# The hi and lo parts of each weight slab placed value by value side by side, in a two-block fp32 transformer kernel on one core

## Chip, core and metric

One core of one Trainium2 chip. The metric is the device time of one launch in microseconds. A DMA engine group feeds SBUF, TensorE multiplies out of SBUF into PSUM, and VectorE, ScalarE and GpSimd do the elementwise work.

## What is computed

The reference runs two blocks over 256 tokens (272 with 16 meta tokens) of width 1024, all in float32:

```
n1 = rmsnorm(h); xr, gr, cq, ckv, kr, g_rnn, g_att = split(n1 @ w_in)
y_rnn = (rg_lru(causal_conv(xr)) * gelu(gr)) @ w_rnn_out
y_att = attention(cq, ckv, kr) @ w_attn_out
h += (sigmoid(g_rnn) * y_rnn + sigmoid(g_att) * y_att) @ w_out
h += peer(rmsnorm(h))          # 16384 experts, 8 heads x 16 chosen per token
x = rmsnorm(h)[:, 16:]
for layer in (0, 1):           # a convolution layer, then an attention layer
    x += 0.5 * rmsnorm(swiglu(rmsnorm(x)))
    x += rmsnorm(mixer(rmsnorm(x)))
    x += 0.5 * rmsnorm(swiglu(rmsnorm(x)))
```

PEER is done densely: scores of all experts, `gelu(n2 @ u.T)`, are multiplied by a sparse coefficient and then by `v`.

## The kernel before

**Weights as a stream.** All weight matrices are cut into 128x128 tiles and laid in HBM in the order in which TensorE uses them (`Plan`), eight tiles to a slab of 512 KB. `Ring` runs the slabs on each engine's own instruction stream: SP loads slab `s` into one of three `raw` buffers (`fetch`), ScalarE rounds it to fp32r (`split_hi`, L392, one instruction of 1024 values to a partition; it waits until TensorE is done with the slab four before), and VectorE, or for every third slab of a long stretch GpSimd, subtracts to get what the rounding left (`split_lo`, L409). TensorE takes tiles with `Weights.take` (L341 to L348).

**Three products to a tile.** Each value is a hi and a lo part, and `mm3` (L323) makes hi*hi, hi*lo and lo*hi: the tile's hi part is loaded twice and its lo part once. Every product is one weight load of 128x128 and one matmul of 256 columns (272 in the first stage). So the tile of weights is the stationary operand and the activations (`n1`, `n2`, `xg`, `bn`, `akv`, `hh`, `o`, `ql`: pairs of hi and lo in fp32r) are moving. In three stretches it is the other way round: the first block's values (`ukv_v`, read as 4 tiles side by side), PEER's `v` (1024 columns, in matmuls of 512) and the last block's values (`wv`). There activations stand in the array, and the slab moves. In PEER's `v` stretch what stands is the coefficients `c`, of which three buffers turn over (`split_coef` on ScalarE and VectorE).

**Where things lie.** `whi0..3` and `wlo0..3` are eight areas of 4096 bytes a partition, one behind the other; a tile is 512 bytes in each, read with a step of 4 bytes. The areas placed after them start as follows, counted from `whi0` and modulo 256 bytes: `hh`, `akv`, `n2` and `c` at 0, `bn` and `xg` (placed from the top of SBUF) at 64; `n1` has rows of 1088 bytes and so takes on 0, 64, 128 and 192.

**Order of the work.** Each engine's order is written out by hand; `ring.to(...)` puts the slab work between the others at fixed places. TensorE's order is: first block (with 192 tiles of `gr`, `g_rnn`, `g_att` as filler between the attention heads), `w_out`, PEER's queries, `u` (128 columns of 8 tiles, with one-hot bf16 products of 64 columns in bursts of 24 that build coefficients), `v` (again with such bursts in its first half), then the second block: feed-forward 0, convolution, feed-forward 1 and 2, attention, feed-forward 3.

Of the kernel before, what the change touches and what calls it, by code (L numbers as in the profile page):

```python
# [14 lines left out]
ACT = mybir.ActivationFunctionType  # L15
ALU = mybir.AluOpType
AX = mybir.AxisListType
BF16 = mybir.dt.bfloat16
F32 = mybir.dt.float32
F32R = mybir.dt.float32r  # L20
# [3 lines left out]
NC = D // 128  # L24
NMETA = 16
NX = 256
# [5 lines left out]
PH, PK, NKEY = 8, 16, 128  # L32
NU = 2 * PH
CW, DWW = 4, 31
SLAB = 8
NRAW, NSPLIT = 3, 4
# [27 lines left out]
TG, NCF = 8, 3  # L64
# [16 lines left out]
class Plan:  # L81
# [23 lines left out]
    def col(self, key, name, c, n=NC):  # L105
        self.run(key, [(name, k, c) for k in range(n)])
# [89 lines left out]
PLAN = Plan()  # L196
NSLAB = PLAN.nslab
# [11 lines left out]
    return (10 <= s <= 18 and s % 2 == 0) or (21 <= s <= 345 and s % 3 == 0) or (417 <= s <= 431 and s % 3 == 0)  # L209

LO_AT = {}
_n = {"lo_v": 1, "lo_p": 0}
# [64 lines left out]
class Kernel:  # L279
# [25 lines left out]
    def place(self, name, shape, dt=F32, top=False):  # L305
# [8 lines left out]
        assert self.low <= self.high, name  # L314
        return self.nc.alloc_sbuf_tensor_at(name, shape, dt, offset=at)

    def col(self, name, c):
        return self.par[:, PCOL[name] + c:PCOL[name] + c + 1]

# [15 lines left out]
class Weights:  # L335
# [5 lines left out]
    def take(self, name, row, c, n=1):  # L341
        k, (s, j) = self.k, divmod(self.pos, SLAB)
        assert j + n <= SLAB and PLAN.order[self.pos:self.pos + n] == [(name, row, c + i) for i in range(n)]
        q, v = LO_AT[s]
        k.P.wait_ge(k.s[q], 1 if self.pos + n <= SLAB // 2 else v)
        self.pos += n
        cols = slice(j * 128, (j + n) * 128)
        return k.whi[s % NSPLIT][:, cols], k.wlo[s % NSPLIT][:, cols]  # L348

    def end(self, ins, pos=None):  # L350
        if (self.pos if pos is None else pos) in PLAN.ends:
# [21 lines left out]
class Ring:  # L373
# [6 lines left out]
    def split_hi(self):  # L380
        k, s, A = self.k, self.his, self.k.A
        self.his += 1
        if self.me is not A:
            return
        A.e.wait_ge(k.raw_in[s % NRAW], 16 * (s // NRAW + 1))
        if s == 0:
            for c in (slice(0, SLAB * 64), slice(SLAB * 64, SLAB * 128)):
                k.s["hi"].inc(k.act(k.whi[0][:, c], k.raw[0][:, c], ACT.Copy))
            return
        if s >= NSPLIT:  # L390
            A.wait_ge(k.s["tiles"], PLAN.count[SLAB * (s - NSPLIT + 1)])
        k.s["hi"].inc(k.act(k.whi[s % NSPLIT][:, :], k.raw[s % NRAW][:, :], ACT.Copy))  # L392

    def split_lo(self):
        k, s, me = self.k, self.los, self.me
        self.los += 1
        if me is k.S:
            return self.fetch(s + NRAW)
        q = LO_AT[s][0]
        if me is not (k.G if q == "lo_p" else k.V):  # L400
            return
        raw, hi, lo = k.raw[s % NRAW], k.whi[s % NSPLIT], k.wlo[s % NSPLIT]
        if s == 0:
            for i, c in enumerate((slice(0, SLAB * 64), slice(SLAB * 64, SLAB * 128))):
                me.wait_ge(k.s["hi"], i + 1)
                k.s[q].inc(me.e.tensor_tensor(lo[:, c], raw[:, c], hi[:, c].bitcast(F32), ALU.subtract))
            return
        me.wait_ge(k.s["hi"], s + 2)
        k.s[q].inc(me.e.tensor_tensor(lo[:, :], raw[:, :], hi[:, :].bitcast(F32), ALU.subtract))  # L409

    def fetch(self, s):
        k = self.k
# [39 lines left out]
def tensors(k):  # L452
    k.H = k.place("H", [128, NC, T])
    k.par = k.place("par", [128, PCOL["wdw"]])
    k.ident = k.place("con", [128, 128])[:, :]
    k.ones = k.place("ones", [128, 128])[:, :]
    k.std = k.place("std", [128, 8])[:, :]
    k.rcol = k.place("rcol", [128, 8])[:, :]
    k.junk = k.place("junk", [128, 1])[:, :]
    k.acc = k.place("acc", [128, NX])[:, :]  # L460
    k.eps6 = k.place("eps6", [128, 1])[:, :]
    k.eps5 = k.place("eps5", [128, 1])[:, :]
    k.half = k.place("half", [128, 6 * NC])
    k.raw = [k.place(f"raw{i}", [128, SLAB * 128]) for i in range(NRAW)]
    k.whi = [k.place(f"whi{i}", [128, SLAB * 128], F32R) for i in range(NSPLIT)]
    k.wlo = [k.place(f"wlo{i}", [128, SLAB * 128], F32R) for i in range(NSPLIT)]
    k.X = [k.H[:, c, NMETA:T] for c in range(NC)]
    low, high = k.low, k.high
    block1_tensors(k)
    k.low, k.high = low, high  # L470
    peer_tensors(k)
    k.low, k.high = low, high
    block2_tensors(k)
# [885 lines left out]
def peer_tensors(k):  # L1359
    p = k.p = Box()  # L1360

    p.iT = [k.place(f"iT{a}", [128, NX, 2], BF16)[:, :, :] for a in range(2)]
    p.gp = k.place("gp", [128, NG, 3, TG, 2], BF16)
    p.io = k.place("iota16", [128, NKEY // 2, 2], BF16)[:, :, :]
    p.c = [k.place("c0", [128, 2, NX], F32R)]
    low = k.low
    p.n2 = k.place("n2", [128, NC, 2, NX], F32R)
    p.kh, p.kl = k.place("kh", [128, 2, NKEY], F32R), k.place("kl", [128, 2, NKEY], F32R)
    p.q2 = k.place("q2", [128, 2, 2, NX], F32R)

    k.low = low
    ohA1 = [k.place(f"ohA{i}", [128, TG, NKEY], BF16)[:, :, :] for i in range(2)]
    ohB1 = [k.place(f"ohB{i}", [128, 3 * TG, HK], BF16)[:, :, :] for i in range(2)]
    oh1 = k.place("oh1", [128, TG, HK], BF16)[:, :, :]
    p.c += [k.place(f"c{i}", [128, 2, NX], F32R) for i in range(1, NCF)]

    act2 = k.place("act2", [128, HK * NX], F32, True)
    high = k.high
    p.xg = k.place("xg", [128, NC, 2, NX], F32R, True)
    p.sqs = k.place("sqs", [128, NC, NX], F32, True)  # L1380
    p.rb = k.place("rb", [128, NX], F32, True)[:, :]

    k.high = high
    act1 = k.place("act1", [128, HK * NX], F32, True)
    p.halves = [act1, act2]
    p.chunks = [(act1, act2)[e // HK][:, e % HK * NX:(e % HK + 1) * NX] for e in range(NKEY)]


    at_ = [0]

    def scr(n, dt=F32):
        a = act2[:, at_[0]:at_[0] + n]
        at_[0] += n
        return a.bitcast(dt) if dt is not F32 else a

    p.sc = scr(2 * NU * NKEY).rearrange("p (a u n) -> p a u n", a=2, u=NU)
    p.t12 = scr(2 * NU * PK).rearrange("p (a u n) -> p a u n", a=2, u=NU)
    p.i12 = scr(2 * NU * PK, U32).rearrange("p (a u n) -> p a u n", a=2, u=NU)
    p.f12 = scr(2 * NU * PK).rearrange("p (a u n) -> p a u n", a=2, u=NU)
    p.cand = [scr(256) for _ in range(2)]  # L1400
    p.cand2 = [scr(256) for _ in range(2)]
    p.rep = [scr(128) for _ in range(2)]
    p.top = scr(NU * PK).rearrange("p (u n) -> p u n", u=NU)
    p.sel = scr(NU * PK, U32).rearrange("p (u n) -> p u n", u=NU)
    p.sab = [scr(NU * PK, U32).rearrange("p (u n) -> p u n", u=NU) for _ in range(2)]
    p.fab = [scr(NU * PK).rearrange("p (u n) -> p u n", u=NU) for _ in range(2)]
    p.hot = scr(4 * PK * PK).rearrange("p (u j a) -> p u j a", u=4, j=PK)
    p.iab = [scr(NU * PK).rearrange("p (u n) -> p u n", u=NU) for _ in range(2)]
    p.gs = scr(NU * PK).rearrange("p (u n) -> p u n", u=NU)
    p.gsum = scr(NU)  # L1410
    p.io128 = scr(NKEY)
    p.kraw = scr(2 * NKEY).rearrange("p (a n) -> p a n", a=2)
    assert at_[0] <= (TAIL - HK) * NX

    bf = act2[:, (TAIL - HK) * NX:].bitcast(BF16)
    part = lambda o, n: bf[:, o * TG:(o + n) * TG].rearrange("p (t i) -> p t i", t=TG)
    ohA0 = [part(i * NKEY, NKEY) for i in range(2)]
    ohB0 = [bf[:, (2 * NKEY + 3 * i * HK) * TG:(2 * NKEY + 3 * (i + 1) * HK) * TG].rearrange("p (t i) -> p t i", i=HK)
            for i in range(2)]
    p.ohA, p.ohB, p.oh1 = [ohA0, ohA1], [ohB0, ohB1], [part(2 * NKEY + 6 * HK, HK), oh1]  # L1420
    p.xg_pair = [(p.xg[:, c, 0, :], p.xg[:, c, 1, :]) for c in range(NC)]
    p.n2_pair = [(p.n2[:, c, 0, :], p.n2[:, c, 1, :]) for c in range(NC)]
    p.c_pair = [(c[:, 0, :], c[:, 1, :]) for c in p.c]


    k.low = low
    p.y = k.place("y", [128, 2, D])
    p.yT = [k.PS[:, 4 + m // 2, NX * (m % 2):NX * (m % 2) + NX] for m in range(NC)]
# [662 lines left out]
def block2_tensors(k):  # L2091
# [12 lines left out]
    c = z.conv = Box()  # L2104
# [2 lines left out]

    def ffn_tensors(i):
        f = Box()
        f.hh = k.place(f"hh{i}", [128, NFF, 2, NX], F32R)  # L2110
        f.gsc, f.sil, f.hf = (k.place(f"{n}{i}", [128, 3, NX]) for n in ("gsc", "sil", "hf"))
        f.x = [(f.hh[:, j, 0, :], f.hh[:, j, 1, :]) for j in range(NFF)]
        return f
# [9 lines left out]
    k.low, k.high = low, high  # L2123
    z.ffn.append(ffn_tensors(1))
    k.low = low
    z.akv = k.place("akv", [128, NC, 2, NX], F32R)
    z.kvn = [(z.akv[:, c_, 0, :], z.akv[:, c_, 1, :]) for c_ in range(NC)]
    low2 = k.low
    z.ffn.append(ffn_tensors(2))
    k.low = low2  # L2130
    a = z.att = Box()
# [1115 lines left out]
```

## Time and profile before

| | |
|---|---|
| median of 3 runs | 2185.61 us (2181.64 to 2186.68) |
| the profiled execution | 2189.28 us |
| its span, first to last instruction | 2187.9 us |
| TensorE, share of the span with a matmul in it | 97%, 17080 matmul records |
| VectorE, ScalarE, GpSimd | 74%, 55%, 26% |
| DMA | 352.86 MB read, 49% of 16 engines |
| mean granted clock of TensorE | 0.990 |

A matmul record lasts from its issue to its last result, so records overlap and a "busy" TensorE says nothing of its pace. The pace is read from the times between starts. Time between the span and the whole execution is 1.4 us.

### The profile page before, as it was taken

To read this page: it belongs to the slowest core of one execution; us is meant where nothing else is said; L and a number is where in the kernel's file an instruction comes from. 1 tells how busy PE (TensorE), PEld (TensorE's weight loads), DVE (VectorE), ACT (ScalarE), POOL (GpSimd) and SP (SyncE) were. 2 spreads that over 40 slices of the span, in tenths; PEclk is the share of its full clock that TensorE was granted. 3 is DMA by queue.
4 is the path that set the end of the run, shared out by engine and by line. 5 is a ranking of instruction groups with operands and counts; after the bars stand their busy time and mean duration, and the time that the engine had idled before them with its cause. 6 is when DMAs were issued, how large, how long until landed. Compare 5 with 4: busy or idle time off the path is not lost.

```text
span 2187.9 us, 41590 instructions
## 1 busy us (share of the span) xinstructions
PE 2129.9 (97%) x17080; PEld 2033.4 (93%) x17080; DVE 1612.8 (74%) x2603; ACT 1195.2 (55%) x2106; POOL 570.7 (26%) x386
## 2 busy tenths in 40 slices
PE   9999999999999999999999999989999999999997
PEld 9898999999999988888889998979999999899997
DVE  7887767798988399975567647968656764788664
ACT  6776656454433444445567755865445544566453
POOL 7432245233222233333333002242001101113001
PEclk9999999999999999999999999999999999999999
DMA  5433455555444554555545554224554555534553
GB/s 172 151 126 106 146 169 168 185 177 188 158 156 151 177 162 159 172 183 192 194 165 184 186 193 133 77 81 153 191 193 144 193 184 193 181 129 159 190 192 114
DMA packets 101131, 357.15 MB, mean 163 GB/s; under 512 B 12048, under 2 KB 15440, under 8 KB 100816
## 3 DMA queue, kind: packets, MB, share of 16 engines
q1 hardware_dynamic: 100080, 352.35, 49.0%
q8 instruction: 136, 2.23, 0.4%
q10 hardware_dynamic: 864, 2.16, 0.3%
q14 instruction: 51, 0.42, 0.1%
HBM read 352.86 MB, written 1.05 MB: 162 GB/s over the span
## 4 chain that ended last, share of the span: by engine, by line
PE 82%; DVE 10%; ACT 3%; issue 2%; DMA 2%; POOL 1%; SPq 0%; POOLq 0%; ACTq 0%; DVEq 0%
PE PS L321 81%; DVE wlo L409 2%; DMA raw<-stream 2%; DVE w L2782 1%; DVE H L2715 1%; ACT whi L329 1%; DVE bn L2666 1%; DVE H L2713 1%; DVE ohA L1877 1%; POOL wlo L409 1%; DVE gate L1223 0%; ACT bsq L329 0%; ACT L329 0%; DVE gate L1234 0%; POOL XC L1304 0%
## 5 line engine op out<-in xcount | busy, mean ns | idle before, releaser
L409 DVE TENSOR_TENSOR wlo<-raw,whi 128x1024 fp32r<-128x1024 f32 x546 | 688.2, 1263 | 225.3 <-ACT whi L329 224.4
L329 ACT ACTIVATE whi<-raw 128x1024 fp32r<-128x1024 f32 (+1 forms) x667 | 698.7, 1050 | 170.0 <-PE PS L321 99.7
L321 PE MATMUL PS<-bn,whi 128*128 128x256 f32 x3328 | 597.1, 281 | 14.7 <-DVE bn L2666 5.0
L321 PEld LDWEIGHTS PS<-bn,whi 128*128 128x128 f32 x3328 | 510.9, 188 | 20.6 <-issue 10.2
L321 PE MATMUL PS<-n,whi 128*128 128x256 f32 (+1 forms) x2784 | 519.1, 288 | 8.0 <-DVE wlo L409 3.7
L409 POOL TENSOR_TENSOR wlo<-raw,whi 128x1024 fp32r<-128x1024 f32 x119 | 325.4, 2734 | 684.8 <-ACT whi L329 684.8
L321 PE MATMUL PS<-bn,wlo 128*128 128x256 f32 x1664 | 460.0, 280 | 0.0
L321 PEld LDWEIGHTS PS<-n,whi 128*128 128x128 f32 x2784 | 438.2, 193 | 12.1 <-DVE wlo L409 3.9
L321 PE MATMUL PS<-n,wlo 128*128 128x256 f32 (+1 forms) x1392 | 396.8, 285 | 0.0
L321 PE MATMUL PS<-whi,c 128*128 128x512 f32 x1024 | 324.2, 393 | 0.6 <-ACT act L329 0.6
L321 PEld LDWEIGHTS PS<-bn,wlo 128*128 128x128 f32 x1664 | 313.4, 188 | 0.0
L321 PEld LDWEIGHTS PS<-n,wlo 128*128 128x128 f32 x1392 | 269.1, 193 | 0.0
L321 PE MATMUL PS<-hh,whi 128*128 128x256 f32 x1408 | 253.6, 283 | 0.0
L321 PEld LDWEIGHTS PS<-whi,c 128*128 128x128 f32 x1024 | 192.3, 188 | 40.0 <-issue 0.7
L321 PEld LDWEIGHTS PS<-hh,whi 128*128 128x128 f32 x1408 | 219.6, 192 | 0.0
L321 PE MATMUL PS<-hh,wlo 128*128 128x256 f32 x704 | 199.2, 283 | 0.0
L321 PE MATMUL PS<-wlo,c 128*128 128x512 f32 x512 | 199.2, 389 | 0.0
L329 ACT ACTIVATE act<-PS 128x256 f32<-128x256 f32 x128 | 49.3, 385 | 210.8 <-PE PS L321 210.7
L329 ACT ACTIVATE c<-act 128x256 fp32r<-128x256 f32 x128 | 53.4, 418 | 188.5 <-PE PS L321 188.4
L332 DVE TENSOR_TENSOR c<-act,c 128x256 fp32r<-128x256 f32 x128 | 87.3, 686 | 91.1 <-ACT c L329 90.5
L321 PEld LDWEIGHTS PS<-hh,wlo 128*128 128x128 f32 x704 | 135.1, 192 | 0.0
L1986 POOL TENSOR_TENSOR acc<-bsq 128x256 f32<-128x256 f32 x12 | 10.2, 850 | 470.2 <-ACT bsq L329 470.2
(355 smaller groups left out, 2918.6 us busy)
## 6 DMA issues: line engine op xcount, KB each, us to landing
raw<-stream SPq DMA_DIRECT2D x666, 512.0 KB, 3.3
abias<-c_alibi ACTq DMA_DIRECT2D x1, 1536.0 KB, 6.9
H<-xt SPq DMA_DIRECT2D x4, 256.0 KB, 6.0
out<-H SPq DMA_DIRECT2D x3, 256.0 KB, 2.2
mask<-c_mask SPq DMA_DIRECT2D x1, 272.0 KB, 6.2
K<-Vh SPq DMA_DIRECT2D x2, 136.0 KB, 4.0
K<-Vl SPq DMA_DIRECT2D x2, 136.0 KB, 4.7
out<-H ACTq DMA_DIRECT2D x2, 128.0 KB, 1.9
```

Of the source, the lines that this page charges most:

```text
L321: return self.nc.tensor.matmul(out, l, r, start=start, stop=stop, skip_group_check=True)
L329: return self.nc.scalar.activation(out, in_, func, **kw)
L332: return self.nc.vector.tensor_tensor(out, x, hi.bitcast(F32), ALU.subtract)
L409: k.s[q].inc(me.e.tensor_tensor(lo[:, :], raw[:, :], hi[:, :].bitcast(F32), ALU.subtract))
L1877: step(vec.tensor_tensor(pairs(p.ohA[half][g % 2]), keys(p.iT[1], NKEY), iota(0, NKEY), ALU.is_equal))
L1986: s["acc"].inc(pool.tensor_tensor(k.acc, sq[:, 0, :] if c == 1 else k.acc, sq[:, c, :], ALU.add))
L2666: s["pre_lo"].inc(k.nc.vector.scalar_tensor_tensor(x[:, c, 1, :], k.X[c], pre_gain(k, pre, c), x[:, c, 0, :].bitcast(F32), ALU.mult, ALU.s ...
L2713: V.step(vec.tensor_tensor(k.X[c], k.X[c], z.rp, ALU.mult))
L2715: s["x_new"].inc(vec.tensor_tensor(k.X[c], k.X[c], z.F[:, c, :], ALU.add))
L2782: ins = vec.scalar_tensor_tensor(c.w[:, q, :], c.u[:, q, t:t + NX], z.wdw[:, j:j + 1], c.w[:, q, :], ALU.mult, ALU.add)
```

## The change

Nothing is added, removed or moved in any engine's instruction stream; operands' addresses and steps change.

1. A slab's two parts share one area of 8192 bytes. For slabs whose tiles stand in the array ("paired"), value `i` of hi is at `8i` and that of lo at `8i + 4`: ScalarE writes and VectorE or GpSimd reads and writes with a step of 8 bytes, and TensorE loads a tile with that step. For slabs up to the end of the first block's values, for PEER's `v` and for `wv` the two parts lie apart as before (`halves`).
2. PEER's coefficients `c0..c2` are laid in pairs too, so the weight loads of the `v` stretch have a step of 8 bytes, while the slab moves with a step of 4.
3. `phase(128)` moves `c`, `n2`, `hh` and `akv` so that they start 128 bytes further, modulo 256, from the start of the slab areas. `bn` and `xg` stay at 64, `n1`, `o` and `ql` stay where they were.

```diff
+def paired(s):
+    streams = [(0, (PLAN.at["v", 1] + 7) // SLAB), (PLAN.at["v_", 0] // SLAB, (PLAN.at["v_", NKEY - 1] + 7) // SLAB),
+               (PLAN.at["wv"] // SLAB, (PLAN.at["wv"] + NC * NC - 1) // SLAB)]
+    return not any(a <= s <= b for a, b in streams)
...
+    def phase(self, n):
+        self.low += (n - self.low + self.weights) % 256
...
-        return k.whi[s % NSPLIT][:, cols], k.wlo[s % NSPLIT][:, cols]
+        return k.split[s][:, cols, 0], k.split[s][:, cols, 1]
...
-        k.s["hi"].inc(k.act(k.whi[s % NSPLIT][:, :], k.raw[s % NRAW][:, :], ACT.Copy))
+        k.s["hi"].inc(k.act(k.split[s][:, :, 0], k.raw[s % NRAW][:, :], ACT.Copy))
...
-        raw, hi, lo = k.raw[s % NRAW], k.whi[s % NSPLIT], k.wlo[s % NSPLIT]
+        raw, hi, lo = k.raw[s % NRAW], k.split[s][:, :, 0], k.split[s][:, :, 1]
...
-        k.s[q].inc(me.e.tensor_tensor(lo[:, :], raw[:, :], hi[:, :].bitcast(F32), ALU.subtract))
+        k.s[q].inc(me.e.tensor_tensor(lo, raw[:, :], hi.bitcast(F32), ALU.subtract))
...
-    k.whi = [k.place(f"whi{i}", [128, SLAB * 128], F32R) for i in range(NSPLIT)]
-    k.wlo = [k.place(f"wlo{i}", [128, SLAB * 128], F32R) for i in range(NSPLIT)]
+    w = [k.place(f"w{i}", [128, 2 * SLAB * 128], F32R) for i in range(NSPLIT)]
+    pairs = [x[:, :].rearrange("p (n q) -> p n q", q=2) for x in w]
+    halves = [x[:, :].rearrange("p (q n) -> p n q", q=2) for x in w]
+    k.split = [(pairs if paired(s) else halves)[s % NSPLIT] for s in range(NSLAB)]
...
-    p.c = [k.place("c0", [128, 2, NX], F32R)]
+    by_part = lambda x: x[:, :, :].rearrange("p t q -> p q t")
+    k.phase(128)
+    p.c = [by_part(k.place("c0", [128, NX, 2], F32R))]
     low = k.low
+    k.phase(128)
     p.n2 = k.place("n2", [128, NC, 2, NX], F32R)
...
-    p.c += [k.place(f"c{i}", [128, 2, NX], F32R) for i in range(1, NCF)]
+    k.phase(128)
+    p.c += [by_part(k.place(f"c{i}", [128, NX, 2], F32R)) for i in range(1, NCF)]
...
+        k.phase(128)
         f.hh = k.place(f"hh{i}", [128, NFF, 2, NX], F32R)
...
+    k.phase(128)
     z.akv = k.place("akv", [128, NC, 2, NX], F32R)
```

## Rows read from the trace of the kernel before

**Rows 1.** The page, busy us of each engine, share of the span, count.
```profile
PE 2129.9 (97%) x17080; PEld 2033.4 (93%) x17080; DVE 1612.8 (74%) x2603; ACT 1195.2 (55%) x2106; POOL 570.7 (26%) x386
```
**Rows 2.** Waits of TensorE, the largest: us in total, times, longest.
```profile
PE PS L321 <- DVE wlo L409: 6.4, 3, 3.7
```
**Rows 3.** Timeline of TensorE from 600.01 us, PEER's `u`, `n2` moving: start us, us, xcount.
```profile
600.01 0.40 PE L321 MATMUL PS<-n,whi 128*128 128x256 f32 x2
...
601.45 0.87 PE L321 MATMUL PS<-act 128*128 128x64 bf16 x24
```
**Rows 4.** The same from 1725.73 us, feed-forward, `bn` moving.
```profile
1725.73 0.28 PE L321 MATMUL PS<-bn,wlo 128*128 128x256 f32 x1
...
1727.14 0.28 PE L321 MATMUL PS<-bn,wlo 128*128 128x256 f32 x1
```
**Rows 5.** The same from 1801.81 us, feed-forward, `hh` moving.
```profile
1801.81 0.40 PE L321 MATMUL PS<-hh,whi 128*128 128x256 f32 x2
...
1802.89 0.40 PE L321 MATMUL PS<-hh,whi 128*128 128x256 f32 x2
```
**Rows 6.** The same from 1000.04 us, PEER's `v`, `c` standing.
```profile
1000.04 0.39 PE L321 MATMUL PS<-wlo,c 128*128 128x512 f32 x1
...
1001.40 0.39 PE L321 MATMUL PS<-wlo,c 128*128 128x512 f32 x1
```
**Rows 7.** The same from 270.07 us, first block, `n1` moving.
```profile
270.07 0.28 PE L321 MATMUL PS<-n,wlo 128*128 128x256 f32 x1
...
271.84 0.28 PE L321 MATMUL PS<-n,wlo 128*128 128x256 f32 x1
```
**Rows 8.** Groups of instructions by form: xcount | busy us, mean ns | idle before.
```profile
L321 PE MATMUL PS<-act 128*128 128x64 bf16 x768 | 27.9, 193 | 0.0
L321 PE MATMUL PS<-bn,whi 128*128 128x256 f32 x3328 | 597.1, 281 | 14.7 <-DVE bn L2666 5.0 <-ACT bn L329 4.5 <-DVE wlo L409 2.7
L321 PE MATMUL PS<-hh,whi 128*128 128x256 f32 x1408 | 253.6, 283 | 0.0
L321 PE MATMUL PS<-whi,c 128*128 128x512 f32 x1024 | 324.2, 393 | 0.6 <-ACT act L329 0.6
L321 PE MATMUL PS<-xg,whi 128*128 128x256 f32 x256 | 48.0, 282 | 0.0
L321 PE MATMUL PS<-akv,whi 128*128 128x256 f32 x256 | 47.7, 285 | 2.0 <-DVE akv L2666 1.2 <-ACT akv L329 0.8
L321 PE MATMUL PS<-o,whi 128*128 128x256 f32 x256 | 45.8, 282 | 0.6 <-DVE o L332 0.6
```
**Rows 9.** Timeline and groups: transposes of 128 columns in float32, first block.
```profile
101.05 0.60 PE L716 MATMUL PS<-con,Sm 128*128 128x128 f32 x4
L716 PE MATMUL PS<-con,Sm x64: 270/272/421, 101.1 to 225.0; 128*128 128x128 f32 x64
```
**Rows 10.** Groups of instructions: the slab's splitting, and two of 512 values on VectorE.
```profile
L329 ACT ACTIVATE whi<-raw 128x1024 fp32r<-128x1024 f32 x665 | 697.5, 1051 | 168.6 <-PE PS L321 99.7 <-DMA raw<-stream 62.9 <-DVE gp L1865 2.1
L409 DVE TENSOR_TENSOR wlo<-raw,whi 128x1024 fp32r<-128x1024 f32 x546 | 688.2, 1263 | 225.3 <-ACT whi L329 224.4
L409 POOL TENSOR_TENSOR wlo<-raw,whi 128x1024 fp32r<-128x1024 f32 x119 | 325.4, 2734 | 684.8 <-ACT whi L329 684.8
L332 DVE TENSOR_TENSOR PT<-PS,PT 128x512 fp32r<-128x512 f32 x16 | 10.8, 676 | 0.8 <-ACT PT L329 0.4
L1890 DVE TENSOR_TENSOR act<-PS,act 128x512 f32<-128x512 f32 x64 | 43.6, 682 | 0.0
```
**Rows 11.** Stretches of time: us, busy us (count) of PE, PEld, DVE, ACT, POOL, clock, DMA share, GB/s.
```profile
450.00:500.00 50.00, 50.00 (x419) 50.00 (x419) 49.69 (x99) 26.48 (x38) 15.51 (x7) 1.00 0.55 179
550.00:600.00 50.00, 50.00 (x593) 49.57 (x593) 49.13 (x55) 20.00 (x30) 13.36 (x5) 1.00 0.47 159
600.00:650.00 50.00, 50.00 (x594) 49.53 (x593) 43.30 (x50) 18.94 (x30) 12.54 (x5) 1.00 0.48 159
650.00:700.00 50.00, 50.00 (x612) 49.57 (x611) 47.93 (x54) 19.78 (x30) 13.24 (x5) 1.00 0.45 149
1500.00:1600.00 100.00, 100.00 (x851) 100.00 (x851) 73.53 (x111) 50.77 (x75) 10.24 (x8) 1.00 0.58 189
```
**Rows 12.** DMA issues: xcount, KB each, median us from issue to landing.
```profile
raw<-stream SPq DMA_DIRECT2D x666, 512.0 KB, 3.3
```

More of the change, by code:

```diff
@@ L387, in split_hi @@
             for c in (slice(0, SLAB * 64), slice(SLAB * 64, SLAB * 128)):
-                k.s["hi"].inc(k.act(k.whi[0][:, c], k.raw[0][:, c], ACT.Copy))
+                k.s["hi"].inc(k.act(k.split[0][:, c, 0], k.raw[0][:, c], ACT.Copy))
             return
@@ L463, in tensors @@
     k.half = k.place("half", [128, 6 * NC])
+    k.weights = k.low
     k.raw = [k.place(f"raw{i}", [128, SLAB * 128]) for i in range(NRAW)]
-    k.whi = [k.place(f"whi{i}", [128, SLAB * 128], F32R) for i in range(NSPLIT)]
-    k.wlo = [k.place(f"wlo{i}", [128, SLAB * 128], F32R) for i in range(NSPLIT)]
+    w = [k.place(f"w{i}", [128, 2 * SLAB * 128], F32R) for i in range(NSPLIT)]
+    pairs = [x[:, :].rearrange("p (n q) -> p n q", q=2) for x in w]
+    halves = [x[:, :].rearrange("p (q n) -> p n q", q=2) for x in w]
+    k.split = [(pairs if paired(s) else halves)[s % NSPLIT] for s in range(NSLAB)]
     k.X = [k.H[:, c, NMETA:T] for c in range(NC)]
```

## The prediction

> **What bounds the kernel now.** I read the engines' shares first: TensorE has a matmul in flight for 97% of the span, VectorE works for 74%, ScalarE for 55% [rows 1]. Then TensorE's waits: the largest releaser costs it 6.4 us in total [rows 2]. So almost nothing outside TensorE sets the time, and the question is TensorE's own pace. Busy time can't give it, since records overlap; the starts can. Each product is one weight load and one matmul, and start to start it takes:
> - `n2` moving: 12 matmuls in 601.45 - 600.01 = 1.44 us, 120.0 ns each [rows 3]
> - `hh` moving: 9 in 1.08 us, 120.0 ns [rows 5]
> - `bn` moving: 12 in 1.41 us, 117.5 ns [rows 4]
> - `n1` moving, first block: 15 in 1.77 us, 118.0 ns [rows 7]
> - `c` standing, 512 columns moving: 6 in 1.36 us, 226.7 ns [rows 6]
>
> From 256 to 512 columns the pace grows by 106.7 ns, 0.417 ns a column, which is the 2.4 GHz level at a granted clock of 1.00 [rows 11]. What is left above the columns' own time is 120.0 - 106.7 = 13.3 ns at 256 and 226.7 - 213.4 = 13.3 ns at 512. The bf16 burst of 64 columns shows how small that can be: 24 matmuls in 0.87 us, of which the last lasts 0.193 [rows 3, 8], so (0.87 - 0.193) / 23 = 29.4 ns each, and 29.4 - 26.7 = 2.7 ns above the columns. So the fp32r products pay 13.3 - 2.7 = 10.6 ns more than the burst does, and with `bn` 10.8 - 2.7 = 8.1 ns.
>
> Two things speak about what these 8 to 11 ns are. They do not shrink when the matmul gets twice as long, so a weight load too long to hide behind the matmul is not it. And they depend on where the moving operand lies: `n2` and `hh`, at 0 modulo 256 from the slabs, give 120.0; `bn`, at 64, gives 117.5. A cost that follows the addresses of two operands points to their two reads meeting in SBUF. The moving read goes at 4 bytes in 0.417 ns. If the weight read takes its 128 values in about the time of the 256 columns, it goes at 4 bytes in 0.83 ns, half as fast in bytes, so the faster one overtakes it again and again, wherever the two begin. With a step of 8 bytes the weight read advances through memory as fast as the moving one, and the distance between them stays what it was at the start. That is what the change would do, and `phase(128)` sets the distance.
>
> **The sum.** No instruction is added or moved, so everything lies in durations.
>
> TensorE. Matmuls that get a stepped weight load, with the lo groups half as many as the hi groups [rows 8]: `bn` 3328 + 1664 and `xg` 256 + 128, together 5376; `hh` 2112; `akv` 384; `c` 1536; `n2` 128 x 8 x 3 = 3072; and in the first block 384 with `o`, 256 tiles x 3 = 768 with `n1`, 126 with `ql` and 42 with `kvl`, together 1320. In all 13,800. If the whole excess goes:
> - 5376 x 8.1 ns = 43.5 us
> - (3072 + 2112 + 384) x 10.6 = 59.0 us
> - 1536 x 10.6 = 16.3 us
> - 1320 x (118.0 - 109.4 = 8.6) = 11.4 us
>
> together 130 us. Bounds: nothing from below if the excess is something else, and a loss if the stepped load is slower (rivals). I take nearly the whole, since the nearest row with no excess, the burst, shows that the array itself does not need it.
>
> What takes some of it back:
> - VectorE. In PEER's `u` stretch it is busy 49.69 of 50 us at 450 to 500 us, and 140.4 of 150 us at 550 to 700 [rows 11]. TensorE would ask for 4.4 us of the first 50 back and about 11 of the later 150; 0.3 and 9.6 are idle there, and not all at the right moment. I take 10 us off here and in the similar first half of `v`.
> - Other waits. Slabs come in every 24 x 0.110 = 2.64 us in place of 2.88. ScalarE needs 1.05 and VectorE 1.26 for each [rows 10], a load lands in 3.3 us with three buffers [rows 12]: one buffer's round is about 3.3 + 1.05 + 1.26 = 5.6 us against 3 x 2.64 = 7.9. That cover holds. At the seams between stages a few slabs will be late: 5 us off.
> - Rest. Products of `n1` lie at all distances, 0 among them, and `bn`'s are at 60 and 64: 7 us off for meetings that stay.
>
> 130 - 22 = 108 us.
>
> ScalarE, VectorE and GpSimd now touch the slab with a step of 8 bytes. Two rows on VectorE bear on it: 512 values written densely take 676 ns, and 512 values read out of PSUM and in `act` at scattered places take 682 [rows 10]. So a step costs VectorE about nothing; for ScalarE no row has a stepped float32 write, and I take 1051 ns as before; its other end is twice the time, still hidden at 55% load, since 2.1 us fit into 2.64 by themselves, though not with the work between them. GpSimd's 2.7 us for every third slab has 8 us.
>
> The sum is made against the profiled execution, 2189.3 us: 2189.3 - 108 = 2081. The median of the three runs lies 3.7 us below that execution, so the forecast for the median is **2078 us**. A difference below 0.2%, some 4 us, can't be told from none.
>
> **Rivals.**
> 1. *Nothing to take away.* The 10 ns belong to every fp32r product, as turn-over between two weight sets. For it: `n1` moves at four distances and still has 118.0 [rows 7], near `bn`'s 117.5. Against it: the difference between 0 and 64. Time: 2186 us, with 4 either way. Chance 0.14. The Trainium skill ("TensorE: Matmul & The Clock Gate", section "Step-by-step: what each phase is for") says that the two reads have SBUF ports of their own and that loading the next tile steals nothing from the running matmul; by that rule this rival holds, and the trace disagrees so far as 120.0 and 117.5 differ by address alone.
> 2. *The stepped weight load is slower* (ends slower). It spreads a tile over 1024 bytes in place of 512. A load of 128 columns has no row of its own below 109 ns: four transposes of 128 columns follow each other in (0.60 - 0.272) / 3 = 109 ns [rows 9], though their columns need only 53. So a load may already be as long as a 256-column product should be, and from that point each nanosecond more is seen: 12,264 products of 256 columns make 12 us of it. If the excess doubles, 13,800 x 10.6 = 146 us more: 2332 us. If the load took twice its time, 218 ns, it would be 12,264 x 98 ns = 1200 us; nothing points there. Small losses of 1 to 3 ns are part of this case. Chance 0.17. The Trainium skill ("SBUF — State Buffer", section "Door 1: The DMA port swizzle") speaks of 16-byte lines that want two hits each; a step of 8 bytes gives just two, so that rule sees no penalty, and no row here can show it.
> 3. *The splitting becomes the bound.* If VectorE's split took twice as long by the step, 546 x 1.07 = 584 us more make 2197 us of work for it, more than TensorE's. In the feed-forward it has 26.5 us idle in 100 with 35 slabs [rows 11], so it decides from 0.76 us more a slab. Time about 2400 us. The 682 ns row speaks against it. Chance 0.05.
>
> **How the numbers follow.** Forecast (excess goes wholly or for the most part): 0.64, with 2055 (all 130 us) to 2165 (a sixth of it) as its own range. Rival 1: 0.14. Rivals 2 and 3: 0.22. Faster takes all of the forecast, same is rival 1, slower the other two. The range reaches from 2055 over no change to 2210, where small losses of rival 2 lie; it leaves out the large ones and a little at the fast end, 2 in 10.
>
> **What would show it.** Right: starts of 256-column products at 109 to 111 ns with `n2`, `hh` and `bn`, 512 columns at 216 to 218, the split rows still at 1051 and 1263 ns, TensorE's waits on `wlo` grown in PEER's `u`. If the start times stay at 118 and 120, rival 1; at 123 or more, or with `bn` alone bad, rival 2; split rows grown and TensorE waiting, rival 3.

## The result and the profile after

| | before | after |
|---|---|---|
| median | 2185.1 us (4 runs) | 2217.0 us (4 runs) |
| ratio | | 1.0146, 95% interval 1.0124 to 1.0168 |
| span of the profiled execution | 2187.9 us | 2215.6 us |

The kernel became 32 us slower; 2078 us was forecast, in a range of 2055 to 2210. First the busy time of the kernel after, to be read against [rows 1]. Then the splitting of slabs between 1500 and 1700 us, in feed-forward, where every slab is paired: ScalarE before and after (the hi and lo parts now share the name `w`).

```profile
PE 2161.4 (98%) x17080; PEld 2072.2 (94%) x17080; DVE 1613.0 (73%) x2603; ACT 1244.3 (56%) x2106; POOL 574.6 (26%) x386
...
L329 ACT ACTIVATE whi<-raw 128x1024 fp32r<-128x1024 f32 x69 | 72.4, 1052 | 31.9 <-PE PS L321 24.7 <-DMA raw<-stream 7.1
L341 ACT ACTIVATE w<-raw 128x1024 fp32r<-128x1024 f32 x66 | 76.0, 1155 | 28.1 <-PE PS L333 23.8 <-DMA raw<-stream 4.2
```

VectorE's split did not change: 1240 ns here against 1241 before, 1262 against 1263 over the whole kernel. ScalarE's takes 1155 ns in place of 1052, so a step of 8 bytes costs its write 10%; its mean over the kernel, 1127 ns, mixes paired slabs with the dense ones of PEER's `v`. GpSimd's mean rose by 50 ns, from 2734 to 2784. None of this adds to the longest of TensorE's waits, 6.4 us before [rows 2]:

```profile
PE PS L333 <- DVE w L421: 6.1, 3, 3.7
```

So, as before [rows 2], TensorE sets the time, by its pace. Its timeline in the kernel after, where one row now holds a whole run of products (start us, us from the first start to the last end, count):

```profile
367.17 181.66 PE L333 MATMUL PS<-n,w 128*128 128x256 f32 x1512
...
999.83 120.50 PE L333 MATMUL PS<-w,c 128*128 128x512 f32 x520
...
1163.14 115.55 PE L333 MATMUL PS<-bn,w 128*128 128x256 f32 x960
...
1506.69 117.15 PE L333 MATMUL PS<-bn,w 128*128 128x256 f32 x960
...
1623.68 64.10 PE L333 MATMUL PS<-hh,w 128*128 128x256 f32 x528
```

A row's time less that of its last matmul, over the count less one, is the pace.

- `bn`, feed-forward 1: (117.15 - 0.28) / 959 = 121.9 ns, and 120.2 in feed-forward 0, against 117.5 [rows 4]
- 512 columns: (120.50 - 0.39) / 519 = 231.4 ns, against 226.7 [rows 6]
- `hh`: (64.10 - 0.28) / 527 = 121.1 ns, against 120.0 [rows 5]
- `n2`, the first 1512 of its 3072 products: (181.66 - 0.28) / 1511 = 120.0 ns, as before [rows 3]

No product got faster by anything near 10 ns. Where the 28 us of span came from can be read off the chain of waits. Two of its pieces, before and after: the last 978 products of the `v` stretch, bursts included, and most of feed-forward 2.

```profile
927.12 203.43 PE PS L321 x978
...
1682.17 183.15 PE PS L321 x1534
```
```profile
935.78 207.47 PE PS L333 x978
...
1699.92 187.52 PE PS L333 x1534
```

This part of `v` took 4.0 us more and feed-forward 2 took 4.4 us more. Feed-forwards 1 and 3 lost about the same. The first product with `n2` starts at 362.53 us before and at 367.17 after, so nearly 5 us were lost ahead of it, in the first block and the queries, and none in the 1512 products that follow.

### The profile page after: what moved, and what is told of

Read it like the earlier page. It is cut to its first block, busy times and chain, and to the rows that moved or that the text cites. A ratio compares the mean times of both kernels' runs of the same rounds, so it can differ in the third digit from the quotient of the medians.

```text
span 2215.6 us, 41590 instructions
## 1 busy us (share of the span) xinstructions
PE 2161.4 (98%) x17080; PEld 2072.2 (94%) x17080; DVE 1613.0 (73%) x2603; ACT 1244.3 (56%) x2106; POOL 574.6 (26%) x386
## 4 chain that ended last, share of the span: by engine, by line
PE 87%; DVE 7%; ACT 3%; issue 2%; POOL 1%; DMA 1%; SPq 0%; POOLq 0%; ACTq 0%; DVEq 0%
PE PS L333 86%; DVE w L421 1%; DVE w L2805 1%; DVE H L2738 1%; DVE bn L2689 1%; DMA raw<-stream 1%; DVE H L2736 1%; POOL w L421 1%; ACT w L341 0%; ACT bsq L341 0%; DVE gate L1250 0%; POOL XC L1320 0%; DVE XR L1189 0%; POOL acc L3067 0%; ACT L341 0%
## 5 line engine op out<-in xcount | busy, mean ns | idle before, releaser
L421 DVE TENSOR_TENSOR w<-raw,w 128x1024 fp32r<-128x1024 f32 x546 | 687.5, 1262 | 227.8 <-ACT w L341 227.2
L341 ACT ACTIVATE w<-raw 128x1024 fp32r<-128x1024 f32 (+1 forms) x667 | 749.9, 1127 | 164.0 <-PE PS L333 103.1
L333 PE MATMUL PS<-bn,w 128*128 128x256 f32 x4992 | 615.8, 285 | 13.9 <-DVE bn L2689 4.8
L333 PEld LDWEIGHTS PS<-bn,w 128*128 128x128 f32 x4992 | 609.9, 197 | 18.4 <-issue 9.6
L333 PE MATMUL PS<-n,w 128*128 128x256 f32 (+1 forms) x4176 | 535.6, 288 | 7.3 <-DVE w L421 3.7
L333 PEld LDWEIGHTS PS<-n,w 128*128 128x128 f32 x4176 | 519.4, 197 | 11.2 <-DVE w L421 3.9
L421 POOL TENSOR_TENSOR w<-raw,w 128x1024 fp32r<-128x1024 f32 x119 | 331.3, 2784 | 690.7 <-ACT w L341 688.7
L333 PE MATMUL PS<-w,c 128*128 128x512 f32 x1536 | 363.7, 395 | 0.6 <-ACT act L341 0.6
L333 PEld LDWEIGHTS PS<-w,c 128*128 128x128 f32 x1536 | 298.0, 196 | 53.4 <-issue 0.7
L333 PE MATMUL PS<-hh,w 128*128 128x256 f32 x2112 | 256.4, 284 | 0.0
```

The source lines that it names most:

```text
L333: return self.nc.tensor.matmul(out, l, r, start=start, stop=stop, skip_group_check=True)
L341: return self.nc.scalar.activation(out, in_, func, **kw)
L421: k.s[q].inc(me.e.tensor_tensor(lo, raw[:, :], hi.bitcast(F32), ALU.subtract))
```

## The experiments

The first two split the change; four measure TensorE's products by themselves; two try what those showed. Times are compared with the kernel before on the same chip. The four kernels of products alone (e3, e4, e7, e8) leave out the computation and write zeros; each stands on a single execution, and together they ran on three chips.

**e1, the pairs alone**

```diff
     def phase(self, n):
-        self.low += (n - self.low + self.weights) % 256
+        return
```

> The change without its moves by 128 bytes: hi and lo are paired, so 13,800 weight loads have a step of 8 bytes, but n2, hh, akv and c stay at 0 modulo 256 from the slabs as in the kernel before. Theory A (the step of 8 itself costs, wherever the moving operand lies): bn still at 120 to 121 ns start to start as after the change, hh and n2 at 121 too, time about 2217 us. Theory B (the distance decides, and 128 is the bad one): bn as after the change, since it did not move, but n2 and hh back at 120.0 or better and the 512-column products at 227 in place of 231: 1536 x 4 ns + 5568 x 1 ns = some 12 us less than the change, about 2205 us. Rival C (with distance 0 the two reads advance together and always meet): n2 and hh at 125 ns or more, 5568 x 5 = 28 us more, about 2245 us.

Measured: 2212.3 us, ratio 1.0121 (1.0104 to 1.0138). Nearly the whole loss is here. From its timeline:

```profile
365.83 181.66 PE L333 MATMUL PS<-n,w 128*128 128x256 f32 x1512
...
999.71 120.56 PE L333 MATMUL PS<-w,c 128*128 128x512 f32 x516
...
1504.87 117.15 PE L333 MATMUL PS<-bn,w 128*128 128x256 f32 x960
...
1621.85 63.52 PE L333 MATMUL PS<-hh,w 128*128 128x256 f32 x528
```

`bn`, which lies where it always did, again has 121.9 ns; 512 columns have (120.56 - 0.39) / 515 = 233.3. Theory B falls, since `c` at its old distance is no better than at 128. Rival C falls too: `n2` and `hh` have 120.0 ns each, not 125. Theory A is near for `bn` and for the total, but not right in its 121 ns for `n2` and `hh`, which keep the 120.0 of the kernel before [rows 3, 5]. So the pairs cost the products that ran under 120 ns, `bn` above all, and the 512-column ones, and took nothing from those that had 120.

**e2, the distance alone**

```diff
-    return not any(a <= s <= b for a, b in streams)
+    return False
...
-    p.c = [by_part(k.place("c0", [128, NX, 2], F32R))]
+    p.c = [k.place("c0", [128, 2, NX], F32R)]
```

and the same for `c1` and `c2`.

> The other half alone: hi and lo lie apart and every weight load has a step of 4 bytes as before, but n2, hh, akv and c start at 128 modulo 256 from the slabs as in the change. Theory A (the step costs): bn at 117.8, the rest near 119, time about 2180 to 2186 us, as before the change. Theory B (the distance 128 is bad by itself, as the unstepped 512-column products of the last block's values hint, which went from 227 to 229 to 233 ns): 512-column products at 231 ns, hh and n2 at 120 to 121, bn unchanged, about 2192 us.

Measured: 2189.6 us, ratio 1.0015 (1.0006 to 1.0025). Timeline of this kernel:

```profile
360.69 179.64 PE L333 MATMUL PS<-n,w 128*128 128x256 f32 x1512
...
999.83 120.56 PE L333 MATMUL PS<-w,c 128*128 128x512 f32 x516
...
1607.79 62.82 PE L333 MATMUL PS<-hh,w 128*128 128x256 f32 x528
```

The 512-column products lose 6.6 ns by the distance of 128 alone (233.3), near theory B's 231, while `n2` and `hh` gain, as theory A had it: (179.64 - 0.28) / 1511 = 118.7 ns and (62.82 - 0.28) / 527 = 118.7, against 120.0. An estimate from these: 1536 x 6.6 = 10 us lost, 5568 x 1.3 = 7 us gained, which leaves the 3 us measured. So distance does act, at a step of 4 bytes, and in both directions. Losses of e1 and e2 don't add in `v`: 233.3 with either, 231.4 with both.

**e3, products alone.** A kernel of its own: an area of weights and an area of moving values are filled once, then TensorE runs stretches of 96 products, in short

```
mm(out, hi, x0); mm(out, hi, x1); mm(out, lo, x0)     # hi, lo: 128 values at step bytes; x0, x1 at `distance` from the weights
```

> Leaves out the whole computation and writes zeros: a kernel of TensorE products alone, in stretches of 96 (4 tiles of results x 8 rows x hi*x0, hi*x1, lo*x0), one stretch after the other, with a small bf16 product between as a mark. Stretches 2 to 9: weight step 4 bytes, moving operand at 0, 32, 64, 96, 128, 160, 192, 224 modulo 256 from the weights; 10 to 17: the same with step 8; then step 16 at 0 and 64, step 32 at 0 and 64; 512 columns with step 4 at 0, step 8 at 0 and at 128; hi loaded in place of lo; the moving operand with a step of 8 bytes, weights with 4 and with 8; bf16 with steps of 2 and 4 bytes; bf16 with 512 columns. Theory A (each step of the weight read through a further line costs): step 8 some 1 to 3 ns above step 4 at every distance, step 16 and 32 more. Theory of the prediction (meetings of two reads): with step 8 some distances at 109 to 111 ns, others at 120 or more, step 4 at 118 to 120 everywhere; bf16 at 109.5. Rival (fixed cost of an fp32r product): 118 to 120 in all fp32r stretches.

Timeline rows, in order: step 4 at 0, 32, 64; step 8 at 0; steps 16 and 32 at 0; then step 4 and step 8 with 512 columns at 0; last a moving operand with a step of 8 bytes and weights at 4, and bf16 with weight steps of 2 and 4 bytes.

```profile
42.92 11.77 PE L50 MATMUL PS<-moving,weight 128*128 128x256 f32 x96
54.77 11.46 PE L50 MATMUL PS<-moving,weight 128*128 128x256 f32 x96
66.31 11.15 PE L50 MATMUL PS<-moving,weight 128*128 128x256 f32 x96
...
136.09 11.78 PE L50 MATMUL PS<-moving,weight 128*128 128x256 f32 x96
...
231.45 22.68 PE L50 MATMUL PS<-moving,weight 128*128 128x256 f32 x96
...
276.96 23.47 PE L50 MATMUL PS<-moving,weight 128*128 128x256 f32 x96
...
323.90 22.05 PE L50 MATMUL PS<-moving,weight 128*128 128x512 f32 x96
346.02 22.68 PE L50 MATMUL PS<-moving,weight 128*128 128x512 f32 x96
...
403.22 22.33 PE L50 MATMUL PS<-moving,weight 128*128 128x256 f32 x96
...
448.37 10.65 PE L50 MATMUL PS<-moving,weight 128*128 128x256 bf16 x96
459.10 10.66 PE L50 MATMUL PS<-moving,weight 128*128 128x256 bf16 x96
```

Each pace is (us - 0.28) / 95, with 0.39 for 512 columns, and holds one slow start of about 1 ns a product. Step 4: 120.9 at 0, 117.7 at 32, 114.4 at 64. Step 8: 121.1 at 0, and 121.1 to 122.8 over all of the eight distances. Step 16: 235.8. Step 32: 244.1. bf16: 109.2 with either step, so the excess over the columns' time belongs to the 4-byte products, and it does move with the distance. That much of the prediction's picture holds. What does not is that step 8 frees anything.

**e4, distances mapped.** The same kernel with other stretches.

> Products alone again (the computation is left out, zeros are written), now to map the distance between the moving operand and the weights. Stretches of 96 products after a warm-up of 168: first 64 stretches with weight step 4 bytes and the moving operand at 0, 16, 32 ... 1008 bytes modulo 1024; then at 1088, 2112, 3136, 4160, 64, 64; then 32 stretches with weight step 8 at 0, 32 ... 992; then 32 stretches of 512 columns with weight step 4 at 0, 32 ... 992. In e3 step 4 gave 121 ns at 0, 114.4 at 64 and 118 to 121 elsewhere, while the kernel's bn, at 64 modulo 256 but at 832 modulo 1024, has 117.7. If only the distance modulo 256 counts, 64, 320, 576 and 832 all give 114 to 115, and bn's 117.7 has another cause. If the distance counts further up, they differ, and 832 gives about 117.7. If it is neither (the state in which a stretch begins), the repeats at 64 differ from each other by more than 1 ns. With step 8 the theory that it costs by itself expects no distance below 119; the prediction's theory expects at least one at 111 or less. 512 columns: one distance at 220 or less would be worth 1536 x 7 = 11 us in the kernel.

Timeline rows: step 4 at 0, 112, 128 and 192, then 1088 and 2112, each followed by a row of its later half alone; 512 columns with step 4 at 0, 32 and 64.

```profile
43.16 11.77 PE L43 MATMUL PS<-moving,weight 128*128 128x256 f32 x96
...
125.27 11.20 PE L43 MATMUL PS<-moving,weight 128*128 128x256 f32 x96
136.54 11.65 PE L43 MATMUL PS<-moving,weight 128*128 128x256 f32 x96
...
183.22 11.17 PE L43 MATMUL PS<-moving,weight 128*128 128x256 f32 x96
...
788.70 11.15 PE L43 MATMUL PS<-moving,weight 128*128 128x256 f32 x96
793.79 5.94 PE L43 MATMUL PS<-moving,weight 128*128 128x256 f32 x51
799.93 11.57 PE L43 MATMUL PS<-moving,weight 128*128 128x256 f32 x96
804.74 6.52 PE L43 MATMUL PS<-moving,weight 128*128 128x256 f32 x54
...
1239.62 22.05 PE L43 MATMUL PS<-moving,weight 128*128 128x512 f32 x96
1261.76 22.66 PE L43 MATMUL PS<-moving,weight 128*128 128x512 f32 x96
1284.49 22.26 PE L43 MATMUL PS<-moving,weight 128*128 128x512 f32 x96
```

Step 4: 120.9 ns at 0, 114.9 at 112, 119.7 at 128, 114.6 at 192, and the same again 256 bytes on. Step 8: 121.1 to 122.8 at all of 32 distances. 512 columns: 228.0 at 0, 234.4 at 32, 230.2 at 64, and 0 is the best of all: the kernel before had `c` in the best place. The stretches at 1088 and 2112 are both at 64 modulo 256, yet ran at 114.4 and 118.8. Without the slow start that is (5.94 - 0.28) / 50 = 113.3 and (6.52 - 0.28) / 53 = 117.8 ns. The other eight stretches at 64 modulo 256, four of them in the map, all had the slower pace. So one distance can have two paces.

**e5, nothing paired, 192 for the 256-column operands**

```diff
+    k.phase(192)
     p.n2 = k.place("n2", [128, NC, 2, NX], F32R)
...
+        k.phase(192)
         f.hh = k.place(f"hh{i}", [128, NFF, 2, NX], F32R)
...
+    k.phase(192)
     z.akv = k.place("akv", [128, NC, 2, NX], F32R)
```

and `bn` and `xg`, placed from the top, 128 bytes lower; `c` stays.

> The kernel before with nothing paired, and n2, hh, akv, bn and xg moved to 192 modulo 256 bytes from the slabs (c stays at 0). In e4 step 4 gave, settled, 120.0 ns at 0, 117.8 at 64, 118.7 at 128 and 113.3 at 192, repeating every 256 bytes, and 226.7 for 512 columns at 0. If the distance modulo 256 rules the kernel's products as it ruled those alone: 5568 x (120.0 - 113.3) = 37 us for n2, hh, akv and 5376 x (117.8 - 113.3) = 24 us for bn, xg, together 61 us, less some 8 us that VectorE keeps in PEER: about 2133 us, 2125 to 2150. If the good pace at 192 needs the undisturbed run of products alone (other engines reading and writing SBUF, waits between stages): 118 ns stays, about 2180 us.

Measured: 2153.3 us (2143.8 to 2159.3), ratio 0.985 (0.983 to 0.987): faster than both kernels, by 33 us where some 53 were expected, and just outside the 2125 to 2150 that were given. Its chain of waits:

```profile
1460.89 173.72 PE PS L327 x1522
1648.41 180.26 PE PS L327 x1522
...
1956.26 173.72 PE PS L327 x1522
```

The same 1522 products of feed-forward 3 took 181.46 us before. Here feed-forward 1 and 3 took 173.72 and feed-forward 2, with the same distances, 180.26: the two paces of one distance again, now in the kernel, and a reason why the expected gain came only in part. This trace is of the fastest of the four runs (2143.8 us). That the slower ones, up to 15 us, had more stretches at the slow pace is likely, but no trace shows it.

**e6, the pairs on top of that**

```diff
-        return k.whi[s % NSPLIT][:, cols], k.wlo[s % NSPLIT][:, cols]
+        return k.split[s][:, cols, 0], k.split[s][:, cols, 1]
```

with the slab's areas laid as in the change; `c` is not paired.

> The same distances of 192, and the change's pairing of the slabs on top (weight step 8 bytes; c is not paired and stays at 0). e4 gave 120.0 ns for step 8 at 192, against 113.3 for step 4. Theory (a step of 8 takes the good distances away): 256-column products at 120 ns, 10,944 x 6.7 = 73 us more than the run above, about 2200 us. Theory of the prediction (at a constant good distance the paired weights never meet the moving read): 113 or less, at most the time of the run above.

Measured: 2202.4 us, ratio 1.0067 (1.0051 to 1.0084), 49 us more than e5.

```profile
1155.94 115.55 PE L336 MATMUL PS<-bn,w 128*128 128x256 f32 x960
```

120.2 ns, near the 120 that were expected; the loss of 49 us against e5 is less than the 73 that were, since e5 had not gained all of them. The good distance is worth next to nothing once the weights have a step of 8. The pairs make the whole difference of e5 and e6, since nothing else differs.

**e7, products shorter than the load**

The kernel of e3 with fewer columns to a product.

> Products alone (no computation, zeros written), to see the weight load by itself: matmuls shorter than the load. Stretches of 96, moving operand at 192: 64, 128, 192 and 512 columns, each with weight steps of 4, 8 and 16 bytes; then the moving operand with a step of 8 and 64, 128, 256 columns; then 256 columns with step 4 at 192 and at 64, each entered from stretches at 0, 32, 96, 128, 160 and 224; last bf16 with 64, 128 and 256 columns. Line theory (the weight read costs by the 16-byte lines it touches, 32 lines a load at step 4, 64 at step 8, 128 at step 16, and e3's 233 ns at step 16 is the load itself): at 64 columns 233 ns for step 16, about 117 for step 8, and less for step 4 unless something else holds the load at about 109; 512 columns at step 16 near 234 too, since the load just fits. Rival (the load takes as long at step 8 as at step 4, and only the meetings with the moving read differ): at 64 columns steps 4 and 8 alike. The two paces seen at 64 in e3 and e4 (113.3 and 117.8) should come back by what ran before the stretch, and 192 may show them as well.

The short products brought the granted clock down, so part of this run was measured at half clock. A stretch of time (the clock is the third number from the end), which stands for 60 to 168 us, then timeline rows: 64 columns with steps 8 and 16, 128 with step 4, 192 with step 8, 256 with step 4 at 192 (twice, with one at 64 between), last bf16 with 64 columns.

```profile
60.00:80.00 20.00, 20.00 (x94) 19.87 (x95) 0.00 (x0) 0.00 (x0) 0.00 (x0) 0.50 0.00 1
```
```profile
58.26 20.69 PE L47 MATMUL PS<-moving,weight 128*128 128x64 f32 x96
79.07 22.61 PE L47 MATMUL PS<-moving,weight 128*128 128x64 f32 x96
101.81 20.74 PE L47 MATMUL PS<-moving,weight 128*128 128x128 f32 x96
...
180.79 11.61 PE L47 MATMUL PS<-moving,weight 128*128 128x192 f32 x96
...
358.01 11.57 PE L47 MATMUL PS<-moving,weight 128*128 128x256 f32 x96
...
427.92 11.57 PE L47 MATMUL PS<-moving,weight 128*128 128x256 f32 x96
...
451.43 11.17 PE L47 MATMUL PS<-moving,weight 128*128 128x256 f32 x96
...
625.77 2.97 PE L47 MATMUL PS<-moving,weight 128*128 128x64 bf16 x96
```

At 0.50 of the clock, the 1.2 GHz level, 64 columns with step 16 need (22.61 - 0.42) / 95 = 234 ns, as 256 columns did at full clock in e3 (235.8). So this time does not follow TensorE's clock, which points to the reads from SBUF. At half clock step 8 has (20.69 - 0.40) / 95 = 214 ns, and so has step 4 (20.74 us, 128 columns): there the two are alike, as the rival said, and nearly twice what a dense load takes at full clock (112, e8). So this half of the run cannot tell the theories apart. From 182 us on the clock is at 1.00, and with 192 columns step 8 has 119 ns.

Two of the 256-column rows are both step 4 at 192, entered from a stretch at 0 (118.8 ns) and from one at 96 (114.6). What ran before seems to pick the pace, but the stretch just before does not do it alone: step 4 at 64 behind a stretch at 32 had 114.4 ns in e3 and 118.8 here, on another chip.

The bf16 row has (2.97 - 0.19) / 95 = 29 ns a product, each with a weight load of 128 values. So a bf16 load takes no more than 29 ns, about a quarter of what e8 shows for fp32r.

**e8, the load at full clock**

As e7, with 192 products of 256 columns ahead of each stretch.

> Products alone (no computation, zeros written), as the run of short products but with 192 products of 256 columns ahead of each stretch, so that TensorE's granted clock stays full, and only 24 short products to a stretch. In that run a stretch of 192 columns paced 118.3 ns with weight step 8 and, once the clock had risen, 111.7 with step 4. First 224, 208 and 192 columns, each with step 4 at distance 192 and 0 and step 8 at distance 192 and 0; then 256 and 512 columns with steps of 8, 12 and 16 bytes at 192. Line theory (the load reads 32, 64, 96 or 128 lines of 16 bytes at 1.82 ns a line, which is 233 / 128): step 8 stays at 117 to 120 whatever the columns, step 4 goes down to 107 to 113; at 256 columns step 12 gives 175 and step 16 gives 233; at 512 columns both hide behind the matmul, 227 to 240. Rival (only meetings, the load itself as fast at step 8): steps 4 and 8 alike within 2 ns when the matmul is shorter, and step 12 no simple multiple.

Timeline rows: 192 columns at distance 192 with step 4 and with step 8 (the later 14 and 15 products of their stretches), then 256 columns with steps 8, 12 and 16.

```profile
279.29 1.73 PE L44 MATMUL PS<-moving,weight 128*128 128x192 f32 x14
...
331.98 1.94 PE L44 MATMUL PS<-moving,weight 128*128 128x192 f32 x15
...
383.90 11.79 PE L44 MATMUL PS<-moving,weight 128*128 128x256 f32 x96
...
419.14 16.92 PE L44 MATMUL PS<-moving,weight 128*128 128x256 f32 x96
...
459.51 22.89 PE L44 MATMUL PS<-moving,weight 128*128 128x256 f32 x96
```

Step 12 runs at (16.92 - 0.28) / 95 = 175 ns, step 16 at 238, step 8 at 121. A tile read with a step of 12 bytes touches 96 lines of 16 bytes, one with a step of 16 touches 128: 175 / 96 = 1.82 ns and 238 / 128 = 1.86 ns a line. For the 64 lines of a step of 8 bytes that makes 117 to 119 ns. With 192 columns, whose own time is 80 ns, step 4 has (1.73 - 0.27) / 13 = 112 ns and step 8 (1.94 - 0.28) / 14 = 119. The paces are much the same at 208 and 224 columns, so here it is the load that sets them. That the cost goes by lines and not by the bytes spanned is borne out by e3: a step of 32 spans twice as much as one of 16 but touches 128 lines too, and took 244 ns against 236.

The line theory's values came nearly true: step 8 at 117 to 120 (119, and 121 at 256 columns with the slow start), step 4 at 107 to 113 (112), step 12 at 175, step 16 at 233 (238 with the slow start), and 227 to 240 at 512 columns (231, 235 and 241). But 512-column products grow with the step although the load fits into them, so it does not hide without cost. And lines alone do not make the dense load: its 32 lines would be 58 ns, and it takes 112. It is bound by something that follows TensorE's clock, since it takes 214 ns at the 1.2 GHz level (e7).

## Why the prediction was wrong

**The bound was right.** TensorE's own pace sets the time before and after; its waits stayed at 6 us for the largest, and the splits with a step of 8 bytes were covered, ScalarE's 103 ns more included.

**That the excess follows the addresses was right**, and so is that not every product has it: bf16 has 109.2 ns, and step 4 moves between 114.4 and 121 ns by distance (e3, e4). Rival 1, a fixed 10 ns for every fp32r product, is refuted by that.

**The step that failed** is the sentence "With a step of 8 bytes the weight read advances through memory as fast as the moving one, and the distance between them stays what it was at the start", and with it the whole sum of 130 us. It let the load with a step of 8 still take its 128 values in about the time of the 256 columns. That load is itself longer, 117 to 122 ns past the slow start at every distance tried and with 256 down to 192 columns (e3, e4, e8), and that is more than the 109 ns that the sum wanted for the whole product. At 256 columns it becomes the bound: no row of 256 columns with a step of 8 ran under 120. In place of a gain of 8 to 11 ns for each of 13,800 products, `bn` lost about 3 to 4 ns, the 512-column products 5, `hh` 1, and `n2` kept its pace.

**The row that carried the sum did not fit.** The "nearest row with no excess, the burst" is bf16, and a bf16 weight load takes no more than 29 ns (e7). A dense fp32r load takes 112 (e8). So even the layout before could not have reached the 109 ns a product that the burst was taken to allow; the best pace that any fp32r stretch of 256 columns had is 113.3.

**It was rival 2 that came**, with its mechanism as told: a load near the length of the matmul, where each nanosecond more is seen. It had a chance of 0.17 and a price of 146 us by doubling the excess, or "Small losses of 1 to 3 ns"; the loss was 32 us. Its sign, "with `bn` alone bad", is nearly what came. The range reached to 2210 for the small losses and was passed by 7 us. The row that should have raised its chance stood in the prediction, four transposes at 109 ns [rows 9], for a load alone: there was no room for it to grow by a tenth. Rival 3 did not come, as VectorE's split kept its time; its price was mis-added, since twice 1.26 us would make 546 x 1.26 = 688 us more and not 584.

**The terms.** The pairs cost 26 us (e1), `phase(128)` 3 (e2), together 32. The 3 us of e2 are the difference of a gain with `n2` and `hh` and a greater loss in `v`: the change took dense `c` away from 0, the only one of the eight mapped distances at which 512-column products have their best pace (e4).

**The two rules that the rivals named.** The Trainium skill's page "SBUF — State Buffer", section "Door 1: The DMA port swizzle", asks for two hits to a 16-byte line, and so sees no penalty at a step of 8 bytes. The measurements differ: a weight load with two values to a line takes 117 to 120 ns where one with four takes 112 (e8), and a moving fp32r operand with a step of 8 bytes doubles the product, (22.33 - 0.28) / 95 = 232 ns (e3). That a new line costs something, which the same passage of the Trainium skill has, agrees with e8; that two hits absorb it does not, for TensorE and 4-byte values. The Trainium skill's page "TensorE: Matmul & The Clock Gate", section "Step-by-step: what each phase is for", has the two reads independent. For bf16, tried at distance 0 alone, these runs agree (109.2 ns); for fp32r they do not, since the pace moves by 6 ns with the distance alone.

**What stays open.** Whether the two reads meet in SBUF at all, where, and why the period is 256 bytes; what picks one of two paces at 64 and 192, and why `bn`, at the same addresses, has 120.2 ns in feed-forward 0 and 121.9 in 1; why 512-column products lose 5 to 7 ns with a step of 8 although the load fits into them with room to spare. An untested thought on the last: 512 moving values of 4 bytes also cover 128 lines, and their usual 233 ns is what 128 lines of a stepped load took. A kernel that forces the fast pace was not tried.

## What to carry to other kernels

When TensorE's pace is within a tenth of the length of its weight load, nothing may be done to the layout of the weights that touches more lines: measure the load alone, with matmuls shorter than it, and enough long ones ahead to keep the clock at its upper level (e7 lost it, e8 kept it). Take the rows for such an argument from the same type of number, as a bf16 load says nothing of an fp32r one. Keep the 4-byte operands dense, and then choose the distance between the moving operand and the weights modulo 256 bytes by a small kernel of products alone; in this one that was worth 1.5% (2153 us) with no instruction changed. A picture of two streams that keep step is worth testing at one more step size before it carries a sum: a step of 16 would have shown at once that a stepped load gets longer.

## What the runs showed of the hardware

- An fp32r weight load of 128 values with stepped addresses costs about 1.82 ns a touched 16-byte line at full clock: 175 ns at a step of 12 bytes, 236 to 238 at 16, 117 to 120 at 8 (e3, e8). The dense load takes 112. At the 1.2 GHz level a step of 16 still takes 234 ns, while dense and a step of 8 both take 214. A bf16 load takes no more than 29 ns at full clock.
- 256-column fp32r products with dense weights have paces of 113 to 120 ns past their slow start, by the distance of the operands modulo 256 bytes; bf16 ones 109.2.
- One distance can have two stable paces, 113.3 and 117.8 ns, and the stretch before does not settle alone which it is; in the kernel that made 173.72 or 180.26 us for the same 1522 products.
- ScalarE writes 1024 fp32r values with a step of 8 bytes in 1155 ns, densely in 1052; VectorE shows no difference (1240 against 1241).
